# Where a normalised token lives (SBUF or PSUM) and which engine does a quarter of the weighted row sums, in a two-layer decoder step on one core

## The reference

```python
def one(xb):                                     # a block of 128 tokens
    q = (xb @ w_q).astype(f32).reshape(128, 8, 2, 128)
    s = einsum('bhcd,hcnd->bhcn', q, sub_keys)   # 2 x 128 scores for each head
    sv, si = top_k(s, 16)
    cand = sv[:, :, 0, :, None] + sv[:, :, 1, None, :]      # 256 pairs
    fv, fi = top_k(cand, 16)
    eid = take_along(si[0] * 128 + si[1], fi)    # 16 experts of 16384
    g = softmax(fv)
    hpre = einsum('bd,bhkd->bhk', xb, u_tab[eid])           # dot products
    a = gelu(hpre) * g
    return einsum('bhk,bhkd->bd', a, v_tab[eid])            # weighted row sums
```

## Time and profile before

| | |
|---|---|
| median of 3 runs | 4367.6 us (4362.62 to 4372.01) |
| span of the profiled execution | 4356.4 us |
| around the span, to the median | 11.2 us |
| busy: PE, DVE, POOL, ACT | 64%, 65%, 60%, 14% |
| expert retrieval of layer 0 and 1 | about 425 to 2165 us and 2570 to 4340 us |
| moved by DMA | 1267.52 MB, mean 291 GB/s |

### The profile page before, as it was taken

How to read it: one execution, slowest core, us unless ns; L and a number is a source line. 1 busy time by engine, 2 the same in 40 slices (tenths; PEclk the granted TensorE clock), 3 DMA queues, 4 the chain that set the end, 5 groups by cost and what they waited for, 6 DMA issues and landing times.

```text
span 4356.4 us, 41077 instructions
## 1 busy us (share of the span) xinstructions
PE 2784.1 (64%) x7573; PEld 1355.0 (31%) x7573; DVE 2837.7 (65%) x6064; ACT 601.9 (14%) x1614; POOL 2601.7 (60%) x2313
## 2 busy tenths in 40 slices
PE   1498366666656656766778863666666566666566
PEld 1354223233322323322344442232232223322222
DVE  7902777777767777766334347767777677677754
ACT  2110111111111111111122111111111111111011
POOL 2000277777777777776600014778777677777774
PEclk9699688888878888888999976888888888888899
DMA  1540399999999999999900134999999899999997
GB/s 44 44 194 26 121 362 372 370 357 370 379 334 354 374 347 351 368 382 409 398 1 0 52 127 159 364 360 352 356 362 373 328 362 368 342 353 365 359 402 299
DMA packets 355457, 1267.52 MB, mean 291 GB/s; under 512 B 39292, under 2 KB 52092, under 8 KB 351868
## 3 DMA queue, kind: packets, MB, share of 16 engines
q0 software_dynamic: 331776, 1208.11, 73.9%
q1 hardware_dynamic: 23508, 57.71, 4.7%
HBM read 1261.31 MB, written 4.82 MB: 291 GB/s over the span
## 4 chain that ended last, share of the span: by engine, by line
PE 33%; DVE 19%; issue 19%; DMA 14%; POOL 9%; ACT 3%; DVEq 1%; SPq 1%; POOLq 0%; ACTq 0%
PE ps L1370 20%; DMA arena<-in_peer_v,idxv 7%; DMA arena<-in_peer_u,idxu 5%; POOL arena L1577 5%; POOL arena L1565 4%; PE ps L1318 3%; DVE arena L723 2%; DVE arena L712 2%; DVE arena L424 2%; PE ps L1444 2%; PE ps L1459 2%; ACT arena L1064 1%; DVE arena L657 1%; DVE picked L660 1%; PE ps L1340 1%
## 5 line engine op out<-in xcount | busy, mean ns | idle before, releaser
L1370 PE MATMUL ps<-arena 128*128 128x512 f32 x3584 | 1900.8, 679 | 1175.1 <-ACT arena L1064 811.4
L1565 POOL DMA_INDIRECT arena<-in_peer_u,idxu x1152 | 1261.1, 1095 | 1141.8 <-issue 736.0
L712 DVE CUSTOM_DVE_ANT_0 arena<-arena 128x1024 bf16<-128x1024 f32 x1152 | 1387.8, 1226 | 630.6 <-DMA arena<-in_peer_u,idxu 545.7
L1577 POOL DMA_INDIRECT arena<-in_peer_v,idxv x1152 | 1304.7, 1133 | 451.8 <-issue 312.5
L1370 PEld LDWEIGHTS ps<-arena 128*128 128x128 f32 x3584 | 733.4, 216 | 2239.7 <-issue 2114.3
L1064 ACT ACTIVATE arena<-ident,av 128x128 f32<-128x128 f32 x768 | 259.5, 394 | 673.4 <-DVE av L706 423.4
L723 DVE SCALAR_TENSOR_TENSOR arena<-arena,av 128x1024 f32 (+1 forms) x256 | 328.4, 1283 | 6.7 <-DMA arena<-in_peer_v,idxv 6.3
L1340 PE MATMUL ps<-arena 128*128 (+1 forms) x1280 | 300.2, 389 | 10.0 <-DMA arena<-in_peer_wq 5.2
L1340 PEld LDWEIGHTS ps<-arena 128*128 128x128 f32 x1280 | 248.2, 196 | 69.9 <-issue 29.3
L622 DVE MAX8 top<-arena 128x8 f32<-128x128 f32 x128 | 37.0, 289 | 175.0 <-ACT arena L1043 174.7
L1318 PE MATMUL ps<-arena 128*128 128x512 f32 (+1 forms) x320 | 139.7, 599 | 4.4 <-DMA arena<-in_w_glu 4.4
(11 more groups left out here) (214 smaller groups left out, 1966.2 us busy)
## 6 DMA issues: line engine op xcount, KB each, us to landing
arena<-in_peer_u,idxu POOLq DMA_INDIRECT x1152, 6.3
arena<-in_peer_v,idxv POOLq DMA_INDIRECT x1152, 6.3
arena<-in_peer_wq SPq DMA_DIRECT2D x4, 4096.0 KB, 19.8
arena<-in_w_glu SPq DMA_DIRECT2D x2, 4096.0 KB, 13.3
arena<-kern SPq DMA_DIRECT2D x8, 512.0 KB, 22.0
arena<-in_w_q SPq DMA_DIRECT2D x1, 4096.0 KB, 22.9
arena<-in_w_o SPq DMA_DIRECT2D x1, 4096.0 KB, 41.8
arena<-in_gains SPq DMA_DIRECT2D x6, 512.0 KB, 17.5
```

Of the source, the lines that this page charges most:

```text
L712: dve.tensor_tensor_reduce(JUNK[:, k % 2, :], UROWS[:, k % NU_RING, :], XCUR, 1.0, 0.0, ALU.mult, ALU.add, hp[:, par, k:k + 1]).then_inc(S ...
L1370: mm = pe.matmul(ps[:, half, :], DIAG[:, i % 4, :], VROWS[k % NV_RING][:, half * 512:(half + 1) * 512], start=(starts and i == 0), stop=Fa ...
L1565: pool.indirect_dma_start(UROWS[:, k % NU_RING, :], None, tab_u, bass.IndirectOffsetOnAxis(ap=idxu[:, par, k:k + 1], axis=0))\
L1577: pool.indirect_dma_start(VROWS[k % NV_RING], None, tab_v, bass.IndirectOffsetOnAxis(ap=idxv[:, par, k:k + 1], axis=0))\
```

## The change

1. `XCUR`, which the dots read, is now PSUM banks 6 and 7. The two places for queries are both in bank 4 (`QP`), and the two for transposed queries and scores both in bank 5 (`QTP`); scores are written over the transposed queries, which have been copied out by then.
2. All 16 V rows of every slot are products on TensorE. `add_row` and the lists of rows go, a quarter is four rows everywhere, and the V gathers wait for products only.

```diff
-PE_ROWS = [k for k in range(TOPK) if k % 4 != 3]
-DVE_ROWS = [k for k in range(TOPK) if k % 4 == 3]
...
 def products_before(j):
...
-    n = len(PE_ROWS)
-    return n * PACKED + TOPK * (j - PACKED) if isinstance(j, int) and j > PACKED else n * j
+    return TOPK * j
...
-        XCUR = area(20480, D)
...
+        XCUR = ps[:, 6:8, :].rearrange("p a b -> p (a b)")
+        QP = ps[:, 4, :].rearrange("p (a n) -> p a n", a=2)
+        QTP = ps[:, 5, :].rearrange("p (a n) -> p a n", a=2)
...
-                def add_row(t, j, par, k):
...
-                    S.wait(dve, "rows_added", len(DVE_ROWS) * j + i)
-                    gate(dve, v_in[k % NV_RING], 16 * (2 * j + k // NV_RING + 1) + L * 16 * 2 * SLOTS)
-                    row = H[:, bass.ds(t, 1), :].rearrange("p a d -> p (a d)")
-                    dve.scalar_tensor_tensor(row, VROWS[k % NV_RING], av[:, par, k:k + 1], row,
-                                             ALU.mult, ALU.add).then_inc(S["rows_added"], 1)
...
                     def dots(a, b):
                         for k in range(a, b):
                             dot(j, par, k)
-                            for kv in DVE_ROWS:
-                                if adds and k == min(kv + 1, TOPK - 1):
-                                    add_row(before, j - 1, 1 - par, kv)
...
-                act.copy(QN[:, par, :], ps[:, 4 + par, 0:2 * P]).then_inc(S["q_copied"], 1)
+                act.copy(QN[:, par, :], QP[:, par, :]).then_inc(S["q_copied"], 1)
...
-                    for i in range(quarter * n, quarter * n + n):
-                        S.wait(act, "products", products_before(j) + i - 3)
-                        act.activation(DIAG[:, i % 4, :], (ident if rows == PE_ROWS else fold)[:, :], ACT.Copy,
-                                       scale=av[:, par, rows[i]:rows[i] + 1]).then_inc(S["diags"], 1)
+                    for k in range(quarter * 4, quarter * 4 + 4):
+                        S.wait(act, "products", products_before(j) + k - 3)
+                        act.activation(DIAG[:, k % 4, :], (fold if packed else ident)[:, :], ACT.Copy,
+                                       scale=av[:, par, k:k + 1]).then_inc(S["diags"], 1)
...
-                    for i in range(quarter * n, quarter * n + n):
-                        k = rows[i]
-                        S.wait(pe, "diags", products_before(j) + i + 1)
+                    for k in range(quarter * 4, quarter * 4 + 4):
+                        S.wait(pe, "diags", products_before(j) + k + 1)
...
-                    if k_before in rows:
-                        S.wait(pool, "products", products_before(before) + rows.index(k_before) + 1)
-                    else:
-                        S.wait(pool, "rows_added", len(DVE_ROWS) * before + DVE_ROWS.index(k_before) + 1)
+                    S.wait(pool, "products", products_before(before) + k_before + 1)
```

More of the change, by code:

```diff
@@ L70 @@
 PACKED = HEADS * FULL
-PE_ROWS = [k for k in range(TOPK) if k % 4 != 3]
-DVE_ROWS = [k for k in range(TOPK) if k % 4 == 3]
-def pe_rows(j):
-    return list(range(TOPK)) if isinstance(j, int) and j >= PACKED else PE_ROWS
 def products_before(j):
-    n = len(PE_ROWS)
-    return n * PACKED + TOPK * (j - PACKED) if isinstance(j, int) and j > PACKED else n * j
+    return TOPK * j
 def gate(eng, sem, value):
@@ L286, in build @@
         counts = {"xt_copied": 2 * TILES, **dict.fromkeys(per_tile, TILES), **dict.fromkeys(per_head, HEADS * TILES),
-                  **dict.fromkeys(per_slot, SLOTS), **dict.fromkeys(("diags", "products"), products_before(SLOTS)),
-                  "dots": TOPK * SLOTS, "rows_added": len(DVE_ROWS) * PACKED}
+                  **dict.fromkeys(per_slot, SLOTS), **dict.fromkeys(("diags", "products", "dots"), TOPK * SLOTS)}
         peer_sem = {n: sem(n) for n in counts}
@@ L738, in slot @@
                     r = j + 8
-                    adds = not first and len(pe_rows(j - 1)) < TOPK
-                    before = t - 1 if first_head else t
                     def dots(a, b):
@@ L1037, in qt_copy @@
                     S.wait(act, "sc_ready", r - 1)
-                    act.copy(QT[:, par].rearrange("p a n -> p (a n)"), ps[:, 6 + par, 0:2 * P]).then_inc(S["qt_copied"], 1)
+                    act.copy(QT[:, par].rearrange("p a n -> p (a n)"), QTP[:, par, :]).then_inc(S["qt_copied"], 1)
                 def sc_copy(r, par):
@@ L1042, in sc_copy @@
                     S.wait(act, "routed", r - 1)
-                    act.copy(SC[:, par].rearrange("p a n -> p (a n)"), ps[:, 6 + par, 256:512]).then_inc(S["sc_copied"], 1)
+                    act.copy(SC[:, par].rearrange("p a n -> p (a n)"), QTP[:, par, :]).then_inc(S["sc_copied"], 1)
                 def exps(t):
@@ L1055, in diags @@
                 def diags(j, par, quarter):
-                    rows = pe_rows(j)
-                    n = len(rows) // 4
+                    packed = isinstance(j, int) and j >= PACKED
                     if quarter == 0:
                         S.wait(act, "weights", j + 1)
-                    for i in range(quarter * n, quarter * n + n):
-                        S.wait(act, "products", products_before(j) + i - 3)
-                        act.activation(DIAG[:, i % 4, :], (ident if rows == PE_ROWS else fold)[:, :], ACT.Copy,
-                                       scale=av[:, par, rows[i]:rows[i] + 1]).then_inc(S["diags"], 1)
+                    for k in range(quarter * 4, quarter * 4 + 4):
+                        S.wait(act, "products", products_before(j) + k - 3)
+                        act.activation(DIAG[:, k % 4, :], (fold if packed else ident)[:, :], ACT.Copy,
+                                       scale=av[:, par, k:k + 1]).then_inc(S["diags"], 1)
                 def slot(t, h, par, route, first_head, first):
@@ L1359, in products @@
                 def products(t, j, quarter, starts):
-                    rows = pe_rows(j)
-                    n = len(rows) // 4
                     if starts and quarter == 0:
                         S.wait(pe, "h_done", t)
-                    for i in range(quarter * n, quarter * n + n):
-                        k = rows[i]
-                        S.wait(pe, "diags", products_before(j) + i + 1)
+                    for k in range(quarter * 4, quarter * 4 + 4):
+                        S.wait(pe, "diags", products_before(j) + k + 1)
                         gate(pe, v_in[k % NV_RING], 16 * (2 * j + k // NV_RING + 1) + L * 16 * 2 * SLOTS)
                         for half in range(2):
-                            mm = pe.matmul(ps[:, half, :], DIAG[:, i % 4, :],
+                            mm = pe.matmul(ps[:, half, :], DIAG[:, k % 4, :],
                                            VROWS[k % NV_RING][:, half * 512:(half + 1) * 512],
-                                           start=(starts and i == 0), stop=False, skip_group_check=True)
+                                           start=(starts and k == 0), stop=False, skip_group_check=True)
                         mm.then_inc(S["products"], 1)
@@ L1571, in gather_v @@
                     before, k_before = (j, k - NV_RING) if k >= NV_RING else (j - 1, k - NV_RING + TOPK)
-                    rows = pe_rows(before)
-                    if k_before in rows:
-                        S.wait(pool, "products", products_before(before) + rows.index(k_before) + 1)
-                    else:
-                        S.wait(pool, "rows_added", len(DVE_ROWS) * before + DVE_ROWS.index(k_before) + 1)
+                    S.wait(pool, "products", products_before(before) + k_before + 1)
                     pool.indirect_dma_start(VROWS[k % NV_RING], None, tab_v,
```

10 lines of the change are left out of this document (3 added, 7 removed).

## The result

The changed kernel takes **4245.7 us** (median of 4 runs, 4233.24 to 4255.93) against 4367.1 for the kernel before on the same chip (4362.62 to 4372.01): a ratio of 0.972, 95% interval 0.9699 to 0.9741. That is 121 us less where 50 were forecast. The direction and the range were right; the size was not.

What follows compares the result with a forecast made beforehand. A loop through VectorE, ScalarE and TensorE was taken to bound regular slots, going from 43.4 to 43.2 us; -83 (regular slots) + 35 (first slots) - 2 (tile ends) = -50 us gave 4318 us, range 4210 to 4395.

Steps and rivals of the forecast that it cites:

- The head: Regular slot from its start until VectorE runs on the copied scores: 18.7 us before, some 22.8 after.
- the tail: Regular slot from the copied scores to the next slot's start: 23.9 us before, 20.3 after three VectorE additions less.
- Rival 3: TensorE runs the added rows at half clock, 1.7 us more per slot: slower, 4410 us; chance 0.14.
- Rivals 2 and 6: 2: PSUM dots dearer by 0.06 us, 4350 us, chance 0.09; 6: PSUM dots still hold GpSimd, 4355 us, chance 0.07.
- The 35 us: Layer 1's extra VectorE waits before the idxu copy, 43.5 against 8.3 us, expected to go with the shorter loop body.
- rival 1: The branch wait stays dear in one layer: 35 us more, 4353 us; chance 0.15.
- 5 of the first tile, taken alike: Each layer's five regular first-tile slots given the gain of the other 18: 1.4 us each in layer 0, 2.2 in layer 1.
- rival 4: TensorE stays at full clock because it idles less: 119 us less, 4199 us; chance 0.07.
- slots that end a tile: Last slots of tiles: lose the same 3.6 us and gain the same 3.4, -2 us in all.
- the first two of a layer: Slots 0 and 1 of each layer, four in all: forecast to change by 0.
- The head's +3.4 us: Two more rows on TensorE ahead of the scores, 1.72 us each at full clock, lengthen the loop by 3.4 us.
- +5.9 us for the first slot of a tile: First slots of tiles 1 to 3: 5.4 us for four more rows, 0.5 for the token copy; +35 us over six.

Runs made afterwards that it cites:

- The slot with the scores ahead: Changed kernel with regular slots' query transposes and scores ahead of quarter 0 on TensorE, their copies ahead of gelu on ScalarE: 4134.3 us, ratio 0.9456.
- The held-back run: Changed kernel, but TensorE begins a regular slot's queries only when dot 13 of the slot before is done: 4247.9 us.
- the lengthened kernel: Changed kernel with 22 one-column memsets per regular slot on VectorE ahead of the first `best`: 4302.5 us, ratio 0.9857.

## Why the prediction was right and wrong

**Right: what bounds a regular slot.** The head took 22.0 to 23.8 us (22.8 forecast), the tail 20.2 to 20.7 (20.3), the slot 43.45 (43.2), equal in both layers within 0.2. The slot with the scores ahead shows directly that it was this loop: with the scores out of it, the slot falls to about the DMA limit of 41.1 us. The 36 slots gave 56 of 65 us. Quarter 0 took 8.5 to 10.1 us, 9.5 on average, just what the sum had (7.8 + 1.7); the 9 us missing are 0.25 a slot, spread over the head (23.05 on average) and the tail (20.4), with no one cause. Rival 3 (rows at half clock, slower than before) fell: quarter 1 takes 7.11 us, 1.78 a row.

**Right: PSUM costs the dots nothing, and frees GpSimd.** 1219 against 1226 ns; gathers 0.94 us against 1.10 and 1.13, and 0.98 and 1.00 with the token in PSUM but the four additions still there. Rivals 2 and 6 fell. The Trainium skill's page "SBUF — State Buffer", section "SBUF: two separate sides", describes a port pair that VectorE and GpSimd share and that an instruction holds to its end, so that the other blocks. The trace agrees in kind: with both operands of the dots in SBUF a gather took 1.10 to 1.12 us, with one in PSUM 0.94. The page limits the hold by two SBUF inputs to a GpSimd instruction that reads SBUF. A gather here takes its indices from SBUF (`idxu`, `idxv`), so it may be such an instruction; no run separates this.

**Right: the branch.** The 35 us went, with the shorter loop (rival 1 fell), but the reason given was not exact: the code of the two layers is not the same, a pass of the loop has 303 to 310 instructions in layer 1 and 299 to 306 in layer 0. Within layer 1 the wait went with the length in all 14 traces; a shift by 128 instructions changed nothing (41.9 us of 43.7). The window of two 16 KiB pages, of the Trainium skill's "Runtime: NRT & Kernel Launch", section "Instruction fetch mechanics", makes place count as well as length. The runs fit an effect of length; of place the one shift shows none.

**Wrong, the largest part: "5 of the first tile, taken alike".** That step carried the 43.2 us of tiles 1 to 3 over to ten slots of which the sum used no row. They took 41.0 and 42.1 us: 39 us saved, not 18. The reason is rival 4, in these slots alone: there DMA is at its limit (409 GB/s), the rows reach TensorE one at a time, in layer 0 it idles 1.3 to 2.3 us ahead of quarter 0, and quarter 0 keeps 2.4 GHz. With quarter 0 at 7.1 us the head is 20.5 us and the tail without a wait 20.0, together 40.5, less than DMA's 41.1. In tiles 1 to 3 rows 8 to 15 are all there after the long first slot; TensorE does them in one run, idles 6.65 us, starts at 1.2 GHz, and the loop needs 43.4 us. My argument against rival 4, that 6 us of idleness remain ahead of quarter 0, was right for tiles 1 to 3 and was not checked for the first.

A first tile can go either way, at the full clock or like tiles 1 to 3. All ten slots of the changed kernel went at the full clock but the last three of layer 1 (quarters 0 of 8.8, 8.6 and 9.5 us). The held-back run went like tiles 1 to 3 in layer 0 and at the full clock in layer 1, in 215.1 and 203.9 us. In the lengthened kernel one quarter 0 of 8.8 us in layer 0 was followed by quarters of 7.1 again. What tips it is open, and so the 39 us hold some luck: with both layers like tiles 1 to 3 they would be about 25, by the 215.1 us (an estimate).

**Wrong: slots taken at nothing.** The slots that end a tile (-24 us, forecast -2) and the first two of a layer (-17.5, forecast 0) were priced by TensorE's and VectorE's edits alone. But late rows had their share in them too. With the token alone in PSUM they give 13 and 7 us. The clearest is the slot at the end of tile 3 in layer 0, in which 10 MB of weights and masks are loaded beside the gathers: 71.9 us before, 62.8 after, 64.1 with the token alone in PSUM. In slot 1 of a layer VectorE waits 11 us for a U row in the head and reaches `best` after the scores are there, so fewer additions in the tail are a plain gain: 51.2 to 45.7 us in layer 0, and 45.5 with the 16 rows alone. The head's +3.4 us, which I set against it everywhere, doesn't exist there.

**Wrong: +5.9 us for the first slot of a tile.** It was 3.9. The rows cost nearly what they should: against the kernel with the token alone in PSUM, whose first slots sum to 296.9, the change's 327.7 is 5.1 us each, where I had 5.4. What I left out is that these slots gain 1.3 us each from GpSimd's release, in spite of the longer copy: late U rows stood ahead of `weigh` in some of them, and quarter 0, which began 5.9 us into the slot in tiles 2 and 3 of layer 0, now begins at 4.5.

By terms: 21 us too little in the first tile, 22 in the tile ends, 17.5 in the first two slots, 12 in first slots, 2 elsewhere, less 9 too much in the stretches, are the 66 us between -50 and -116. The mechanisms were on the list; what failed was carrying one slot's balance over to the 28 slots of other kinds, with rows of only one of them in the sum.

## What to carry to other kernels

When a steady slot has been worked out, open one slot of every other kind (first tile, first and last slot of a tile, the one with a weight load) before its balance is carried over: here the first tile, the tile ends and the first two slots of each layer, 22 slots, held 80 of the 116 us of span. Two halves of a change that remove different limits of the same loop must be priced together, as the largest of the limits that remain. An engine's idle gap just ahead of a critical burst can cost more than the gap: it is worth filling it, or moving what the others wait for (here the scores) ahead of the burst.

## What the runs showed of the hardware

- A quarter of four rows (16 matmul instructions) took 9.42 us after TensorE had idled 6.65 us and 7.10 after 2.31 us, but also 8.80 after 2.52 us, so the last gap alone does not tell it; filling the gap with 4.46 us of unused matmuls, in a program that was otherwise the same, saved 83 us.
- The five regular slots of a first tile ran at a mean granted clock of 0.94 in one layer and of 1.00 in the other of the same execution (215.1 and 203.9 us). With the 16 rows alone TensorE waited 100 times for V rows in tiles 1 to 3 of layer 0 (73.7 us in all, where the changed kernel has no such wait), and its clock there was 0.94 to 0.96 in the two stretches read, against 0.91.
- The wait at VectorE's loop end (5.7 to 5.9 us each in the lengthened kernel) came with 310 to 316 instructions in a pass of layer 1's loop and not with 305 to 310 in layer 0's; what else tells the layers apart is open.
- The copy of the token to PSUM took 1228 ns (mean of ten), that to SBUF 694.
